# A Mamba-2 scan turned over: y computed channels by tokens, and the decay rows on ScalarE

## The reference, cut to what matters

```
a_cum  = cumsum(a)                                  # per head, inside a chunk
decay  = exp(a_cum[l] - a_cum[s])   for s <= l, else 0
cb     = C_l . B_s                                  # per group
y_diag = (cb * decay) @ x_dt                        # inside the chunk
state' = exp(sum a) * state + sum_s B_s exp(a_end - a_cum[s]) x_dt[s]
y_off  = exp(a_cum[l]) * (C_l . state)              # state at the chunk's start
y      = y_diag + y_off + xs * d_skip
out    = rms_norm(y * silu(z)) @ w_out
```

## Time and profile before

| what | us |
|---|---|
| median of 3 runs (lowest, highest) | 1703.84 (1703.0, 1709.6) |
| the profiled execution, its own time | 1705.06 |
| its span | 1703.3 |
| TensorE busy in the span | 1599.9 |
| VectorE busy | 1223.3 |
| ScalarE busy | 640.5 |
| GpSimd busy | 524.0 |

### The profile page before, as it was taken

How to read it: one execution, slowest core, us unless ns; L and a number is a source line. 1 busy time by engine, 2 the same in 40 slices (tenths; PEclk the granted TensorE clock), 3 DMA queues, 4 the chain that set the end, 5 groups by cost and what they waited for, 6 DMA issues and landing times. The chain is left out here.

```text
span 1703.3 us, 25597 instructions
## 1 busy us (share of the span) xinstructions
PE 1599.9 (94%) x7334; PEld 1255.8 (74%) x7334; DVE 1223.3 (72%) x2255; ACT 640.5 (38%) x1075; POOL 524.0 (31%) x754
## 2 busy tenths in 40 slices
PE   6999999999999999999999882899999999999997
PEld 5778888878888788888887772667776677667774
DVE  6658868768778588687786847566776677766773
ACT  5333232322322232323332331545554455545551
POOL 2222121131221311212312102234454544544454
PEclk9999999999999999999999985899999999999999
DMA  4121121121121212211212625699999999999972
GB/s 151 47 73 51 54 71 38 45 69 44 56 69 44 70 44 56 69 39 45 81 31 73 228 97 212 223 348 372 369 374 375 370 374 374 373 365 360 360 298 78
DMA packets 142989, 292.65 MB, mean 172 GB/s; under 512 B 21340, under 2 KB 71948, under 8 KB 142896
## 3 DMA queue, kind: packets, MB, share of 16 engines
q1 hardware_dynamic: 127904, 266.29, 44.6%
q0 software_dynamic: 14992, 25.22, 4.2%
HBM read 291.81 MB, written 25.30 MB: 186 GB/s over the span
## 5 line engine op out<-in xcount | busy, mean ns | idle before, releaser
L1709 ACT ACTIVATE gu_hi<-w_gu 128x1024 fp32r<-128x1024 f32 x256 | 272.5, 1066 | 312.1 <-PE g_ps L1752 208.1
L1806 DVE TENSOR_TENSOR gu_lo<-w_gu,gu_hi 128x1024 fp32r<-128x1024 f32 x256 | 305.3, 1221 | 79.3 <-ACT gu_hi L1709 69.9
L1027 PE MATMUL proj<-uTh,wl 128*128 128x512 f32 x768 | 309.9, 404 | 6.7 <-issue 6.7
L1029 PE MATMUL proj<-uTh,wh 128*128 128x512 f32 x768 | 302.0, 393 | 0.0
L1028 PE MATMUL proj<-uTl,wh 128*128 128x512 f32 x768 | 301.9, 393 | 0.0
L450 POOL TENSOR_TENSOR wl<-raw,wh 128x512 fp32r<-128x512 f32 x96 | 128.6, 1358 | 392.4 <-ACT wh L511 392.4
L1770 PE MATMUL y<-w_d,hT 128*128 128x512 f32 x512 | 225.1, 592 | 1.1 <-DVE hT L1834 1.1
L1770 PEld LDWEIGHTS y<-w_d,hT 128*128 128x128 f32 x512 | 94.9, 190 | 108.5 <-issue 107.1
L1027 PEld LDWEIGHTS proj<-uTh,wl 128*128 128x128 f32 x768 | 145.8, 190 | 37.1 <-issue 7.4
L1029 PEld LDWEIGHTS proj<-uTh,wh 128*128 128x128 f32 x768 | 145.7, 190 | 31.8
L1028 PEld LDWEIGHTS proj<-uTl,wh 128*128 128x128 f32 x768 | 145.9, 190 | 28.7
(11 more groups left out here) (249 smaller groups left out, 2979.0 us busy)
## 6 DMA issues: line engine op xcount, KB each, us to landing
w_gu<-in_moe_w_gate_dram SPq DMA_DIRECT2D x128, 512.0 KB
w_gu<-in_moe_w_up_dram SPq DMA_DIRECT2D x128, 512.0 KB
w_d<-in_moe_w_down_dram SPq DMA_DIRECT2D x128, 512.0 KB
raw<-in_ssd_w_in_dram SPq DMA_DIRECT2D x96, 256.0 KB, 3.5
E<-acum_dram SPq DMA_DIRECT2D x64, 256.0 KB, 3.5
raw<-in_ssd_w_out_dram SPq DMA_DIRECT2D x32, 256.0 KB, 2.9
hacc<-in_x_dram SPq DMA_DIRECT2D x8, 512.0 KB, 7.5
u_dram<-xbc SPq DMA_DIRECT2D x8, 512.0 KB, 3.3
```

Source lines behind the costliest of these rows:

```text
L1027: nc.tensor.matmul(out, al, bh, start=start, stop=False)
L1029: return nc.tensor.matmul(out, ah, bh, start=False, stop=stop)
L1709: nc.scalar.activation(wh[:, j % RING, :], weights.gate_up(b, j), ACT.Copy).then_inc(w_hi, 1)
L1806: vec.tensor_tensor(wl[:, j % RING, :], weights.gate_up(b, j), wh[:, j % RING, :].bitcast(F32), ALU.subtract).then_inc(w_lo, 1)
```

## The change

y is now computed channels by tokens at once. The state term takes the state as the stationary operand, in two halves of 128 channels, and C as the moving one. In the decay products `xdt` of one head (64 columns) is stationary and the masked decay matrix (128 columns) moves; the heads of a pair write to the lower and upper 64 partitions. `turn_y` and its semaphore are gone, and the gate reads `ysb` directly.

The factor exp(acum) is now a function of the column, not of the partition. ScalarE computes it from the broadcast rows `E` into a new tile `EE`, one exp for each half of the partitions. The subtraction and the clamp at 0 go from VectorE to ScalarE: relu(acum_s - acum_l), and the exp takes its negative. All of it stands where `exp_e` stood, ahead of the copies and of `copy_b`.

A group's first chunk has no state term, no `EE`, a copy in place of the y sum and a copy as state. Its last chunk has no transposed B, no `xds`, no update and no new state (before, the state was set to zero there); its `prep` waits for TensorE's `tcb_done` instead of ScalarE's `btok_done`. The counts of the semaphores change accordingly (`states`).

The diff, cut to its core:

```
+        def states(n):
+            return n if n < NT else n - 1
 ...
-            def exp_e(G, c):
-                wait(act, sub_steps, G, 32, 4 * c + 4)
+            def decay_rows(G, c):
+                wait(act, e_loaded[c % 2], G, 16 * NT // 2, 16 * (c // 2 + 1))
+                if c % NT == 0:
+                    return
+                wait(act, y_steps, G, 2 * NT - 1, 2 * (c - 1) - 1 if c > 1 else 0)
+                for h in range(2):
+                    half_p = slice(h * HEAD_DIM, (h + 1) * HEAD_DIM)
+                    rows_h = E[half_p, c % 2].rearrange("p (t q) l -> p q t l", q=2)[:, h]
+                    nc.scalar.activation(EE[half_p, c % 2], rows_h, ACT.Exp).then_inc(ee_done, 1)
+
+            def decay_between(G, c):
+                a = pick(acum, G) if c < 8 else pick(acum, nxt(G))
+                if c % NT:
+                    wait(act, ee_done, G, 2 * (NT - 1), 2 * states(c))
+                for r in range(R):
+                    er = E[:, c % 2, r, :]
+                    nc.scalar.activation(er, er, ACT.Relu, bias=a[:, 0, c % 8, r:r + 1], scale=-1.0).then_inc(relu_done, 1)
+                wait(act, relu_done, G, 32, 4 * c + 4)
                 e = E[:, c % 2].rearrange("p r l -> p (r l)")
-                nc.scalar.activation(e, e, ACT.Exp).then_inc(exp_done, 1)
+                nc.scalar.activation(e, e, ACT.Exp, scale=-1.0).then_inc(exp_done, 1)

             def copy_b(G, c):
+                if c == NT - 1:
+                    return
 ...
                     if c < NT - 1 or not last:
-                        exp_e(G, c + 1)
+                        decay_rows(G, c + 1)
+                        decay_between(G, c + 1)
 ...
-            def sub_e(G, c):
-                wait(dve, e_loaded[c % 2], G, 16 * NT // 2, 16 * (c // 2 + 1))
-                a = pick(acum, G) if c < 8 else pick(acum, nxt(G))
-                for r in range(R):
-                    e = E[:, c % 2, r, :]
-                    vec.tensor_scalar(e, e, a[:, 0, c % 8, r:r + 1], 0.0, ALU.subtract, ALU.min).then_inc(sub_steps, 1)
 ...
             def prep(G, c):
-                wait(dve, btok_done, G, NT, c + 1)
+                if c == NT - 1:
+                    wait(dve, tcb_done, G, NT, c + 1)
+                else:
+                    wait(dve, btok_done, G, NT - 1, states(c) + 1)
 ...
-            def y_and_state(G, c, last_chunk):
+            def y_sum(G, c):
                 wait(dve, y_mm, G, NT, c + 1)
-                wait(dve, yT_done, G, NT, c)
-                vec.tensor_tensor(heads(ysb[:]), heads(y_ps[:, 0, :]), spread(eac, G, c), ALU.mult).then_inc(y_steps, 1)
+                wait(dve, gate_steps, G, 24, 3 * c)
+                if c % NT == 0:
+                    vec.tensor_copy(ysb[:], y_ps[:, 1, :]).then_inc(y_steps, 1)
+                    return
+                vec.tensor_tensor(ysb[:], y_ps[:, 0, :], EE[:, c % 2].rearrange("p t l -> p (t l)"), ALU.mult
+                                  ).then_inc(y_steps, 1)
+                wait(dve, y_steps, G, 2 * NT - 1, 2 * c)
                 vec.tensor_tensor(ysb[:], ysb[:], y_ps[:, 1, :], ALU.add).then_inc(y_steps, 1)
-                new = S[:, (c + 1) % 2, :]
-                wait(dve, st_mm, G, NT, c + 1)
-                if last_chunk:
+
+            def state(G, c):
+                if c == NT - 1:
+                    return
+                new, update = S[:, (c + 1) % 2, :], st_ps[:, 0, :]
+                wait(dve, st_mm, G, NT - 1, states(c) + 1)
+                if c % NT == 0:
                     for j in range(2):
-                        vec.memset(new[:, j * P:(j + 1) * P], 0.0).then_inc(s_steps, 1)
+                        vec.tensor_copy(new[:, j * P:(j + 1) * P], update[:, j * P:(j + 1) * P]).then_inc(s_steps, 1)
                     return
 ...
             def gate(G, k):
-                wait(dve, yT_done, G, NT, k + 1)
+                wait(dve, y_steps, G, 2 * NT - 1, 2 * k + 1)
                 for t in range(2):
                     vec.scalar_tensor_tensor(ygf[:, t, :], xbc[:, par, t, cols], dsk[:, bass.ds(val(G, 2, t), 1)],
-                                             st_ps[:, 1, t * P:(t + 1) * P], ALU.mult, ALU.add).then_inc(gate_steps, 1)
+                                             ysb[:, t * P:(t + 1) * P], ALU.mult, ALU.add).then_inc(gate_steps, 1)
 ...
             def scan(G, c):
-                wait(pe, s_steps, G, 2 * NT, 2 * c)
-                wait(pe, y_steps, G, 2 * NT, 2 * c)
-                nc.tensor.matmul(y_ps[:, 0, :], xbc[:, H[1] % 2, 3, cc * P:cc * P + P], S[:, c % 2, :], start=True, stop=True)
+                wait(pe, y_steps, G, 2 * NT - 1, 2 * c - 1)
+                if c % NT:
+                    wait(pe, s_steps, G, 2 * (NT - 1), 2 * c)
+                    for t in range(2):
+                        nc.tensor.matmul(y_ps[:, 0, t * P:(t + 1) * P], S[:, c % 2, t * P:(t + 1) * P],
+                                         xbc[:, H[1] % 2, 3, cc * P:cc * P + P], start=True, stop=True)
                 wait(pe, m_done, G, NT, c + 1)
                 for r in range(R):
                     q = slice(r * HEAD_DIM, (r + 1) * HEAD_DIM)
-                    mm = nc.tensor.matmul(y_ps[:, 1, q], E[:, c % 2, r, :], xdt[:, c % 2, q], start=True, stop=True)
+                    half_p = slice(r % 2 * HEAD_DIM, (r % 2 + 1) * HEAD_DIM)
+                    mm = nc.tensor.matmul(y_ps[half_p, 1, r // 2 * P:(r // 2 + 1) * P], xdt[:, c % 2, q], E[:, c % 2, r, :],
+                                          start=True, stop=True)
                 mm.then_inc(y_mm, 1)
-                wait(pe, xdt_steps, G, 2 * NT, 2 * c + 2)
-                wait(pe, btok_done, G, NT, c + 1)
-                wait(pe, gate_steps, G, 24, 3 * c)
+                if c == NT - 1:
+                    return
 ...
-            def turn_y(G, c):
-                wait(pe, y_steps, G, 2 * NT, 2 * c + 2)
-                wait(pe, s_steps, G, 2 * NT, 2 * c + 2)
-                for t in range(2):
-                    mm = nc.tensor.transpose(st_ps[:, 1, t * P:(t + 1) * P], ysb[:, t * P:(t + 1) * P], ident[:])
-                mm.then_inc(yT_done, 1)
```

More of the change, by code:

```diff
@@ L154, in mamba @@
         acum = sb("acum", [P, GROUPS, NT, R])
-        eac = sb("eac", [P, GROUPS, NT, R])
+        EE = sb("EE", [P, 2, 2, P])
         dst = sb("dst", [P, GROUPS, NT, R])
@@ L229, in mamba @@
         e_loaded = [sem(f"e_loaded{j}") for j in range(2)]
-        sub_steps = sem("sub_steps")
+        relu_done = sem("relu_done")
         exp_done = sem("exp_done")
@@ L236, in mamba @@
         s_steps = sem("s_steps")
-        yT_done = sem("yT_done")
+        ee_done = sem("ee_done")
         gate_steps = sem("gate_steps")
@@ L632, in _ @@
                 if i == 8:
-                    act.wait_ge(cum_act, 4)
+                    act.wait_ge(cum_act, 3)
                 if t < 4:
@@ L655, in _ @@
                 if i == 6:
-                    exp_e(G0, 0)
+                    decay_rows(G0, 0)
+                    decay_between(G0, 0)
             copy_b(G0, 0)
-            exp_e(G0, 1)
+            decay_rows(G0, 1)
+            decay_between(G0, 1)
             copy_b(G0, 1)
@@ L885, in prep @@
                 vec.tensor_tensor(cbm[:], tp[:, 3, :], tri[:], ALU.mult).then_inc(cbm_done, 1)
-                wait(dve, xdt_steps, G, 2 * NT, 2 * c + 1)
-                wait(dve, st_mm, G, NT, c - 1)
+                if c == NT - 1:
+                    return
+                wait(dve, xdt_steps, G, 2 * NT - 1, c + 1 + states(c))
+                wait(dve, st_mm, G, NT - 1, states(c - 1))
                 vec.tensor_tensor(heads(xds[:, c % 2, :]), heads(xdt[:, c % 2, :]), spread(dst, G, c), ALU.mult
@@ L895, in make_m @@
                 vec.tensor_tensor(E[:, c % 2], E[:, c % 2], cb, ALU.mult).then_inc(m_done, 1)
-            def y_and_state(G, c, last_chunk):
+            def y_sum(G, c):
                 wait(dve, y_mm, G, NT, c + 1)
-                wait(dve, yT_done, G, NT, c)
-                vec.tensor_tensor(heads(ysb[:]), heads(y_ps[:, 0, :]), spread(eac, G, c), ALU.mult).then_inc(y_steps, 1)
-                wait(dve, y_steps, G, 2 * NT, 2 * c + 1)
-                vec.tensor_tensor(ysb[:], ysb[:], y_ps[:, 1, :], ALU.add).then_inc(y_steps, 1)
-                new = S[:, (c + 1) % 2, :]
-                wait(dve, st_mm, G, NT, c + 1)
-                if last_chunk:
+                wait(dve, gate_steps, G, 24, 3 * c)
[5 more added lines that the diff above has]
+                wait(dve, y_steps, G, 2 * NT - 1, 2 * c)
+                vec.tensor_tensor(ysb[:], ysb[:], y_ps[:, 1, :], ALU.add).then_inc(y_steps, 1)
+            def state(G, c):
[4 more added lines that the diff above has]
+                if c % NT == 0:
                     for j in range(2):
-                        vec.memset(new[:, j * P:(j + 1) * P], 0.0).then_inc(s_steps, 1)
+                        vec.tensor_copy(new[:, j * P:(j + 1) * P], update[:, j * P:(j + 1) * P]).then_inc(s_steps, 1)
```

(24 more changed lines are left out.)

13 lines of the change are left out of this document (7 added, 6 removed).

## The result

The changed kernel takes 1771.6 us (median of 4 runs, 1770.9 to 1772.3) against 1705.6 (4 runs, 1703.0 to 1709.6): a ratio of 1.0388 [1.0375, 1.0402], so 66 us slower. The sign and the mechanism were forecast; of the size, only 40 us were.

The account below looks back on a forecast made before the run. Two nearly equal chains bound steps 2 to 6: TensorE's products and the ScalarE-VectorE loop; TensorE alone bounds 7, 8, 1. Losses of 31 (seven groups), 7.5 (last group) and 1.5 (prologue) sum to 40: 1744 us, range 1712 to 1775.

Parts of the forecast that it names:

- The block: Two exps and four relus ahead of the exp in ScalarE's queue: 2.1 us together, bounds 1.6 to 2.7.
- steps 2 to 8: Values of the loop's inner counter c within a head group; steps 2, 4, 6 have a second, left-over convolution.
- The sum: Total predicted loss over the whole kernel: 40 us, from seven loop groups, the last group and the prologue.
- the loss per loop group: Each of the first seven head groups of the scan gets 4.4 us longer, 31 us for seven.
- The last group: Eighth head group, nothing left to project: loop through ScalarE bounds; 4 steps x 2.1, less 0.9, gives 7.5 us.
- the prologue: Ahead of the scan, the added ScalarE work delays the copy of a convolution's input once: 1.5 us lost.
- The clock: Rival: TensorE's clock falls to 1.2 GHz twice in each of seven groups, 25 us less a sixth: 1765; chance 0.13.
- The course over a group: Lateness followed step by step: gates up to 6.3 us late, step 8 5.4 late, 4.4 left per group.
- everything behind the exp in its queue: ScalarE's projection copies and btok move back behind the added passes, and with btok VectorE's xdt, xds and ms.
- the GpSimd hold-up that `xds` had suffered: In step 6 xds took 1.48 us, held up by a GpSimd pass; the hold-up was let hit another instruction.
- TensorE's prices: Per chunk: turns save 0.22 us, state term 0.46, decay products 0.83; 26 us gained if TensorE alone decided.
- The rival with pairs side by side: Decay products of paired heads run together, 0.41 us less per chunk, kept in steps 7, 8, 1: 9 us, 1735; chance 0.08.

Follow-up runs that it names:

- experiment 1: Changed kernel with ScalarE's copy of B (btok) moved ahead of the two exps, four relus and exp in steps 2 to 7: 1713.6 us, ratio 1.0043.
- experiment 4: Kernel before the change, with only the copy of B moved ahead of its exp in steps 2 to 7: 1707.9 us, ratio 1.0018.
- experiment 3: Changed kernel without the two exps into EE and the four relus, decay factors left out of the computation: 1687.2 us, ratio 0.9894.
- experiment 6: Changed kernel with B copied ahead of the exps and relus, and in steps 1, 6, 7 two weight pieces too: 1673.1 us, ratio 0.9806.
- experiment 5: Changed kernel with all four heads' decay products written to the lower 64 partitions, part of y wrong: 1771.8 us in one run.

## Why the prediction was right, and what it missed

**Direction and mechanism: right.** The block stands ahead of `btok`, `xdt` and `ms` come late, TensorE waits for `ms` and for the squares. It is shown by experiment 1, which moves `btok` and changes nothing else, by its control 4, and by 3, which takes the block out.

**The block: right.** 2.28 us against 2.1. The two exps take 0.84 (forecast 0.75), the relus 1.28 (1.26), the waits of ScalarE on itself 0.13 and 0.03 (0.05 each). The group by line and shape in steps 2 to 8:

```profile
L594 ACT ACTIVATE E<-E,acum 128x128 f32<-128x128 f32 x32 | 10.2, 390 | 1.0 <-ACT EE L585 0.2
L585 ACT ACTIVATE EE<-E 64x256 f32<-64x256 f32 x14 | 5.7, 408 | 0.2
```

**The sum: too small by 28 us, and the term that failed is the loss per loop group.** It was forecast at 4.4 us, 31 for seven groups; the square sums come 8.4 later per group, 59 for seven. The last group (+11.8 up to the last square sums, forecast 7.5) and the prologue (-2.6, forecast +1.5) are off by about 4 each and cancel, which is luck. The paragraph on the course over a group, below, takes the 4.0 apart.

That the idle time came out (40 with 26 us less of work stands for 66 of new idle time, and the trace has 64.4) is luck in part too. The waits that the forecast followed, for `ms` and the squares, grew by 49 us; the other 17 are waits for weights, which it put at nothing.

**The clock: a fact, but not the missing term.** TensorE's passes took 39.3 us more than in experiment 6. The rival in the prediction priced two falls in each group at 25 us less a sixth. In the changed kernel steps 3 and 5 take as long with a fall as without, because the wait for `ms` shrinks by what the passes lose (above); in the last group, too, two steps that follow each other take 11.7 us each, at a granted clock of 0.74 and 0.99. Only the one double fall shows, with 1.4 us. No kernel was run in which the clock stays up throughout, so what it is worth in the other steps is argued.

**The course over a group.** Lateness at the start of the square sums of steps 3, 4, 5, 6 and 8 and of the next step 1, counted from step 1: forecast 1.9, 3.6, 5.2, 6.3, 5.4, 4.4; the mean over seven groups 4.0, 5.3, 7.0, 8.3, 9.8, 8.4. Three readings:
- From step 3 to step 6 it grows by 4.3 where 4.4 was forecast. This is the chain of the prediction, and it holds.
- It is 2.1 too low before that. 1.3 of it arises already in step 1. Experiment 1 keeps that (1.6), experiment 6 has none of it (-0.1): the high parts of weights behind the block, then GpSimd's low parts, then the projection. The prediction named "everything behind the exp in its queue" and followed only `btok`. TensorE's waits for `wl` and `wol` grew by 17 us. The other 0.8 came in step 2, where TensorE waited 1.6 to 2.2 us for `ms` in most groups and 0.5 was forecast. In the group of the rows above, one pass of the gate took 1.49 us in place of 0.42, held up beside GpSimd; in the other groups it was not, so the cause stays open there. The wait in that group:

```profile
391.25 0.50 PE L1057 MATMUL out<-woh,yl 128*128 128x512 f32 x1 [1.73 <-DVE ms L967]
```

- From step 6 to 8 it grows by 1.5 where it was to fall by 0.9. These 2.4 us are the largest part of the 4.0; steps 8 and 1 then give 0.4 more back than forecast. `xdt` of step 6 was as free as forecast (0.58 <- `tcb`), but the projection of step 6 waited for a weight (again a piece behind the block: experiment 1 has the wait too, 6 has not) and that of step 7 for `ms` (forecast 0.6):

```profile
457.22 0.49 PE L1057 MATMUL proj<-uTh,wl 128*128 128x512 f32 x1 [1.03 <-POOL wl L454]
...
468.06 0.50 PE L1057 MATMUL out<-woh,yl 128*128 128x512 f32 x1 [1.45 <-DVE ms L967]
```

  And the GpSimd hold-up that `xds` had suffered (1.48 us) now falls on M and on the convolution, as was allowed for:

```profile
454.49 1.47 DVE L918 TENSOR_TENSOR E<-E,cbm 128x512 f32<-128x512 f32 x1
455.89 1.49 DVE L869 TENSOR_SCALAR v<-xr,cw 128x512 f32<-128x512 f32 x1
```

**Last group.** +11.8 against +7.5. Its steps are 11.7 apart, 11.6 forecast. Of the rest 2.4 is a longer wait for a low part of the output weights, again a piece behind the block (3.6 before, the one wait for `wol` in the view above):

```profile
995.07 0.77 PE L1057 MATMUL out<-woh,yl 128*128 128x512 f32 x1 [5.96 <-POOL wol L454]
```

**Prologue: wrong.** 1.5 us were to be lost; the first square sums start at 115.4 in place of 117.9, 2.6 earlier. The start varies, though: in experiment 4, whose prologue is that of before, it is 120.0.

**TensorE's prices.** State term 0.62 (forecast 0.46, upper bound 0.52: outside it), decay products 0.58 (forecast 0.83, bounds 0.42 to 1.04). The rival with pairs side by side was true as a fact; its 9 us can't be seen in the time, and experiment 5 shows why: passes made longer go into the waits. That ScalarE and not TensorE decides is the reason why the errors here cost the forecast little.

**Left open.** What leaving out the state term of the first chunk and the update of the last is worth alone was not tried; it is part of the 18 us of experiment 3. The weight pieces ahead of the block with `btok` left behind it was not run either, so the 95 to 99 us are those of both moves together. Why the clock falls after some waits and not after others of the same length stays open too.

## What to carry to other kernels

Before work is moved to an engine with free time, read what stands behind it in that engine's queue and who waits for each of those entries, not only the nearest: here 43% busy hid two chains, one through `btok` and one through the weights. The same instructions, with what others wait for put first, were 95 to 99 us faster than as they stood. A longer busy time is not yet a longer kernel: before slower passes are put down as a loss, compare the same step with and without them. Here a fall of the clock cost 1.5 to 1.6 us a step where TensorE decided, and nothing where it waited for others anyway.

## What the runs showed of the hardware

- Two 64-column stationary operands, sent to different halves of the output partitions, ran their 128-column fp32 passes at 0.073 us each on average against 0.127 when sent to the same half.
- Four passes of 128 columns (state term, 0.62 us) took longer than two of 256 (0.52).
- The lower clock level followed waits far under the 3.48 us of the earlier trace rows: in step 5 of one group one of 1.36 us, with another of 0.93 nine microseconds earlier. A wait of 1.37 in the same step of the next group, with one of 0.91 as long before it, left the passes at full speed, with 0.62 us for the state term (556.35 above). So the length of one wait does not settle it.
